# Four expert places of the second layer loaded in mid-mixer, between the ring's items

## The reference

```python
for l in range(DEPTH):                      # 2 layers
    hx = modulate(rmsnorm(x_lat, norm1_g[l]), sh1, sc1)      # latent tokens
    hc = modulate(rmsnorm(x_ctx, norm1_g[l]), csh1, csc1)    # context tokens
    # token mixer: keys and values from both, everything else of the last layer from hx alone
    dk, dv, nk, nv, dq, nq, pz, su, sv, gz = split_cols(hx @ w_in, COL_SIZES)
    dk_c, dv_c, nk_c, nv_c = split_cols(hc @ w_in[:, :KV_COLS], COL_SIZES[:4])
    ...                                     # four branches: pool, diff, sgu, na
    proj = einsum('btie,ied->btid', [pool_x, diff_x, sgu_x, na_x], w_br)
    mix = sum(sigmoid(gz) * proj, branches) @ w_out
    x_lat = x_lat + g1 * mix
    hx2 = modulate(rmsnorm(x_lat, norm2_g[l]), sh2, sc2)
    x_lat = x_lat + g2 * ec_moe(hx2, router_w[l], moe_w1[l], moe_w3[l], moe_w2[l])
    ...                                     # the context likewise, if l is not the last
```

## Time and profile before

| | |
|---|---|
| median of 3 runs | 2049.64 us (2046.07 to 2050.02) |
| profiled execution | 2047.61 us, its span 2045.8 us |
| granted TensorE clock, mean | 0.977 |
| PE busy | 1875.7 us (92%) |
| DVE / ACT / POOL busy | 696.7 / 443.1 / 119.0 us |
| HBM read | 563.11 MB, 276 GB/s over the span |
| chain that ended last | PE 66%, DMA 28%, DVE 3% |

### The profile page before, as it was taken

The page is one execution under the profiler, slowest core; times in us unless marked ns, Lnnn a source line. Parts: engine busy times, 40 slices in busy tenths (PEclk is TensorE's granted clock), DMA queues, the critical chain, the costliest instruction groups (busy, mean ns, idle before and its releaser), DMA issues.

```text
span 2045.8 us, 27379 instructions
## 1 busy us (share of the span) xinstructions
PE 1875.7 (92%) x11512; PEld 1096.7 (54%) x11512; DVE 696.7 (34%) x1149; ACT 443.1 (22%) x774; POOL 119.0 (6%) x159
## 2 busy tenths in 40 slices
PE   5999999999999899999889799999998887988787
PEld 3788756667788433333323488877896222222222
DVE  3263354654333422222212444467555010101001
ACT  3322243443222200000000332344433000000000
POOL 2080000000000100000000232000000000000000
PEclk9999999999999999999999899999998999999989
DMA  9423333344447799999999853444679999999997
GB/s 316 137 89 93 90 116 103 119 132 129 147 134 279 315 410 428 429 428 429 428 429 428 254 151 92 124 146 135 210 241 395 406 427 428 427 428 429 428 428 297
DMA packets 206319, 565.58 MB, mean 276 GB/s; under 512 B 9144, under 2 KB 156752, under 8 KB 180880
## 3 DMA queue, kind: packets, MB, share of 16 engines
q1 hardware_dynamic: 203920, 557.72, 70.6%
q0 software_dynamic: 1760, 4.40, 1.2%
q10 hardware_dynamic: 544, 2.10, 0.3%
HBM read 563.11 MB, written 1.07 MB: 276 GB/s over the span
## 4 chain that ended last, share of the span: by engine, by line
PE 66%; DMA 28%; DVE 3%; issue 1%; SPq 1%; ACT 1%; POOL 0%; DVEq 0%; ACTq 0%
PE PS L837 42%; PE PS L1280 16%; DMA e_h<-in_moe_w 13%; DMA arena<-in_moe_w 12%; DMA ring_par<-in_w_mod 2%; PE PS L893 2%; PE PS L1018 1%; PE PS L1223 1%; PE PS L1040 1%; DMA ring_par<-in_w_in 1%; SPq L773 0%; PE PS L1156 0%; PE PS L905 0%; PE PS L1250 0%; POOL small L1716 0%
## 5 line engine op out<-in xcount | busy, mean ns | idle before, releaser
L837 PE MATMUL PS<-hTr,wr 128*128 128x512 f32 (+1 forms) x2688 | 515.5, 348 | 9.6 <-DMA cst<-in_cst 4.4
L837 PEld LDWEIGHTS PS<-hTr,wr 128*128 128x128 f32 x2688 | 428.6, 190 | 77.0 <-issue 6.3
L1280 PE MATMUL PS<-e_h,arena 128*32 128x512 f32 x1312 | 270.1, 619 | 34.4 <-DMA arena<-in_moe_w 16.8
L1280 PE MATMUL PS<-arena 128*32 128x512 f32 x1216 | 264.0, 613 | 27.6 <-DMA arena<-in_moe_w 24.1
L1745 DVE TENSOR_TENSOR wr<-ring_par,wr 128x1024 fp32r<-128x1024 f32 x152 | 189.2, 1245 | 235.2 <-ACT wr L1351 234.9
L1351 ACT ACTIVATE wr<-ring_par 128x1024 fp32r<-128x1024 f32 x152 | 160.5, 1056 | 297.8 <-PE PS L837 268.3
L1280 PE MATMUL PS<-arena,nab 128*32 128x512 f32 x1088 | 199.6, 596 | 9.1 <-DMA arena<-in_moe_w 7.9
L837 PE MATMUL PS<-wr,hTr 128*128 128x512 f32 x816 | 187.5, 390 | 0.0
L837 PEld LDWEIGHTS PS<-wr,hTr 128*128 128x128 f32 x816 | 152.1, 188 | 32.5 <-DVE wr L1745 1.3
L2188 DVE TENSOR_TENSOR x_work<-x_work,PS 128x512 f32<-128x512 f32 x80 | 50.7, 684 | 345.5 <-PE PS L837 345.5
L1280 PEld LDWEIGHTS PS<-e_h,arena 128*32 128x32 f32 x1312 | 73.9, 113 | 168.4 <-issue 154.5
(11 more groups left out here) (193 smaller groups left out, 1647.7 us busy)
## 6 DMA issues: line engine op xcount, KB each, us to landing
arena<-in_moe_w SPq DMA_DIRECT2D x92, 2048.0 KB, 17.3
e_h<-in_moe_w SPq DMA_DIRECT2D x59, 2048.0 KB, 19.0
ring_par<-in_w_in SPq DMA_DIRECT2D x136, 512.0 KB, 4.1
e_wr<-in_moe_w SPq DMA_DIRECT2D x30, 2048.0 KB, 18.0
ring_par<-in_w_mod SPq DMA_DIRECT2D x92, 512.0 KB, 5.2
ring_par<-in_w_br SPq DMA_DIRECT2D x64, 256.0 KB, 4.6
ring_par<-in_w_out SPq DMA_DIRECT2D x16, 512.0 KB, 3.8
ring_par<-in_moe_w SPq DMA_DIRECT2D x4, 2048.0 KB, 16.7
```

The source lines that it names most:

```text
L837: return nc.tensor.matmul(o, a, b, start=first, stop=last)
L1280: ins = nc.tensor.matmul(PS[r:r + CAP, bank + h, :], src[:, k, r:r + CAP], space[:, kk * D + h * 512:kk * D + (h + 1) * 512], start=(k == ...
```

## The change

Only the second layer changes. A list `EARLY_LOADS` names four pieces that are issued inside the mixer's ring, each right behind the chunk that belongs to its unit: n = 5 in unit 2, n = 2 in unit 18, n = 8 in unit 21, n = 0 in unit 26. Each waits for what last used its memory: n = 5 for the key and value chunks, n = 2 and 8 for the end of the attention (`pv`), n = 0 for the 24th projection. n = 1 stays behind `w_out`, with the wait on the low parts of the merged sums (`m_lo`).

So that these places are free, the second layer lays `hTr` out by stream (the latent tokens fill one half, the context's the other; `by_stream`, `tokens_of`, `stream_of`), puts the rounded high parts of branches 2 and 1 in the unused upper columns of units 0 and 1, those of branch 3 in `x_work` (`x_work_r`, where the attention's buffer was), and the merged sums in the unused columns of units 2 and 3. The number and the sizes of the instructions on PE, DVE and ACT stay as they were.

```diff
+EARLY_LOADS = ((), ((2, 5), (18, 2), (21, 8), (26, 0)))
...
+KV_CHUNKS = 4 * (1 + max(i for i, g in enumerate(GROUPS) if g[0] in KV))
...
-        br_hi_of = {i: arena_r[:, u, :].rearrange("p (k t) -> p k t", k=4) for i, u in split_hi.items()}
+        br_hi_of = [{i: arena_r[:, u, :].rearrange("p (k t) -> p k t", k=4) for i, u in split_hi.items()},
+                    {2: arena_r[:, 0, :].rearrange("p (k t) -> p k t", k=4)[:, :, T:],
+                     1: arena_r[:, 1, :].rearrange("p (k t) -> p k t", k=4)[:, :, T:],
+                     3: x_work_r[:, 4 * D + 4 * 512:4 * D + 6 * 512].rearrange("p (k t) -> p k t", k=4)}]
...
-        mT = [x_flat[:, :].rearrange("p (k t) -> p k t", k=KD), x_flat[:, 2 * D:].rearrange("p (k t) -> p k t", k=KD)]
+        mT = [x_flat[:, :].rearrange("p (k t) -> p k t", k=KD),
+              unit_of(2, 2).rearrange("p (k t) -> p k t", k=KD)[:, :, T:]]
+        by_stream = hTr[:, :, :, :].rearrange("p a k t -> p (a k t)").rearrange("p (s a k t) -> p s a k t", s=2, a=2, k=KD)
+
+        def tokens_of(l, part, k, t0, t1):
+
+            if l == 0:
+                return hTr[:, part, k, t0:t1]
+            if t1 - t0 > T:
+                return by_stream[:, :, part, k, :]
+            return by_stream[:, t0 // T, part, k, t0 % T:t0 % T + t1 - t0]
...
-                    if first and turn == 0:
+                    if first and turn == 0 and l == 0:
                         sync.wait_ge(*(projs.at(l, NM) if s < EARLY_SLOTS else mix_sum.at(l, 2 * NT[l])))
+                    elif first and turn == 0:
+                        sync.wait_ge(*(projs.at(l, 3 * KD), m_lo.at(l, KD), pv.at(l, NB[l]), mix_sum.at(l, 2 * NT[l]),
+                                       mix_sum.at(l, 2 * NT[l]), chunk_sum.at(l, KV_CHUNKS))[s])
...
                     else:
                         sync.wait_ge(*pv.at(l, NB[l]))
-                        sync.wait_ge(*m_lo.at(l, KD))
                     sync.dma_start(xspace[e], rows_of(0, n)).then_inc(extra_loaded[e], 16)
...
+                early = EARLY_LOADS[l]
+                for unit, n in early:
+                    upto = [m for m, it in enumerate(items) if it[:3] == ("chunk", l, NW + unit + 2)][0] + 1
+                    load_items(at_item, upto)
+                    at_item = upto
+                    if n < ESLOT:
+                        load_slot(0, n, True)
+                    else:
+                        load_extra(n)
+                load_items(at_item, late)
+                at_item = end
+                done_early = [n for _, n in early]
                 for n in range(EARLY_SLOTS):
-                    load_slot(0, n, True)
-                if EXTRA[l] > 2:
-                    load_extra(ESLOT + 2)
+                    if n not in done_early:
+                        load_slot(0, n, True)
                 load_items(late, end)
                 load_late(l)
                 for n in range(EARLY_SLOTS, ESLOT):
-                    load_slot(0, n, True)
+                    if n not in done_early:
+                        load_slot(0, n, True)
...
```

More of the change, by code:

```diff
@@ L263, in build @@
         par = ring_par[:, NSLOT * 1024:NSLOT * 1024 + P_ALL]
+        with ExitStack() as rounded:
+            x_work_r = sb("x_work_r", [128, 4 * D + 9 * 512], f32r, rounded)
+            arena_r = sb("arena_r", [128, 8, 2048], f32r, rounded)
+            nab_r = sb("nab_r", [128, 8 * 6 * GRID_W], f32r, rounded)
         x_work = sb("x_work", [128, 4 * D + 9 * 512])
@@ L266, in build @@
         work = x_work[:, 4 * D:].rearrange("p (a b) -> p a b", a=9)
-        with ExitStack() as rounded:
-            arena_r = sb("arena_r", [128, 8, 2048], f32r, rounded)
-            nab_r = sb("nab_r", [128, 8 * 6 * GRID_W], f32r, rounded)
         arena = sb("arena", [128, 8, 2048])
@@ L323, in build, with stream_of @@
         x_flat = x[:, :, :].rearrange("p a b -> p (a b)")
-        mT = [x_flat[:, :].rearrange("p (k t) -> p k t", k=KD), x_flat[:, 2 * D:].rearrange("p (k t) -> p k t", k=KD)]
+        mT = [x_flat[:, :].rearrange("p (k t) -> p k t", k=KD),
[7 more added lines that the diff above has]
+            return by_stream[:, t0 // T, part, k, t0 % T:t0 % T + t1 - t0]
+        def stream_of(l, part, ks, s):
+            return hTr[:, part, ks, s * T:(s + 1) * T] if l == 0 else by_stream[:, s, part, ks, :]
         g1b = unit_of(6).rearrange("p (a b) -> p a b", a=2)
@@ L756, in _ @@
                 late = end - NSLOT * len(late_mod(l))
-                load_items(at_item, late)
-                at_item = end
                 G = GE[l]
@@ L965, in _ @@
                             i = three(bank[:, 0:u["tokens"]], wr[:, q % 2, 0, k * 128:(k + 1) * 128],
-                                      wr[:, q % 2, 1, k * 128:(k + 1) * 128], hTr[:, 0, k, 0:u["tokens"]],
-                                      hTr[:, 1, k, 0:u["tokens"]], k == 0, k == KD - 1, False)
+                                      wr[:, q % 2, 1, k * 128:(k + 1) * 128], tokens_of(l, 0, k, 0, u["tokens"]),
+                                      tokens_of(l, 1, k, 0, u["tokens"]), k == 0, k == KD - 1, False)
                         i.then_inc(chunk_sum.sem, 1)
@@ L1079, in _ @@
                                 i = three(PS[:, 5, 0:tok], wr[:, j % 2, 0, k * 128:(k + 1) * 128],
-                                          wr[:, j % 2, 1, k * 128:(k + 1) * 128], hTr[:, 0, k, 0:tok],
-                                          hTr[:, 1, k, 0:tok], k == 0, k == KD - 1, False)
+                                          wr[:, j % 2, 1, k * 128:(k + 1) * 128], tokens_of(l, 0, k, 0, tok),
+                                          tokens_of(l, 1, k, 0, tok), k == 0, k == KD - 1, False)
                             if arg == 1:
@@ L1117, in output @@
                         i = three(PS[:, 2 * m + n, :], wr[:, j % 2, 0, n * 512:(n + 1) * 512],
-                                  wr[:, j % 2, 1, n * 512:(n + 1) * 512], hTr[:, 0, k, m * 128:(m + 1) * 128],
-                                  hTr[:, 1, k, m * 128:(m + 1) * 128], k == 0, k == KD - 1, True)
+                                  wr[:, j % 2, 1, n * 512:(n + 1) * 512], tokens_of(l, 0, k, m * 128, (m + 1) * 128),
+                                  tokens_of(l, 1, k, m * 128, (m + 1) * 128), k == 0, k == KD - 1, True)
                         if k == KD - 1:
@@ L1381, in part_high @@
                     s, kp, _ = pairs[t]
-                    nc.scalar.activation(hTr[:, 0, 2 * kp:2 * kp + 2, s * T:(s + 1) * T],
+                    nc.scalar.activation(stream_of(l, 0, slice(2 * kp, 2 * kp + 2), s),
                                          htmp[:, t % 4, :].rearrange("p (k t) -> p k t", k=2), ACT.Copy)\
@@ L1507, in branch_high @@
                             act.wait_ge(*projs.at(l, HALF))
-                    nc.scalar.activation(br_hi_of[b][:, k, 0:tok], branches[:, b, k, 0:tok], ACT.Copy)\
+                    nc.scalar.activation(br_hi_of[l][b][:, k, 0:tok], branches[:, b, k, 0:tok], ACT.Copy)\
                         .then_inc(branch_hi.sem, 1)
@@ L1549, in _ @@
                     act.wait_ge(*chunk_sum.at(l, NW + NM))
-                    nc.scalar.activation(hTr[:, 0, k, 0:tok], mT[l][:, k, :], ACT.Copy, scale=0.5).then_inc(m_hi.sem, 1)
+                    nc.scalar.activation(tokens_of(l, 0, k, 0, tok), mT[l][:, k, :], ACT.Copy, scale=0.5).then_inc(m_hi.sem, 1)
                     if k == 1:
@@ L1801, in part_low @@
                     dve.wait_ge(*h_hi.at(l, t + 1))
-                    nc.vector.tensor_tensor(hTr[:, 1, 2 * kp:2 * kp + 2, s * T:(s + 1) * T],
+                    nc.vector.tensor_tensor(stream_of(l, 1, slice(2 * kp, 2 * kp + 2), s),
                                             htmp[:, t % 4, :].rearrange("p (k t) -> p k t", k=2),
-                                            hTr[:, 0, 2 * kp:2 * kp + 2, s * T:(s + 1) * T].bitcast(f32),
+                                            stream_of(l, 0, slice(2 * kp, 2 * kp + 2), s).bitcast(f32),
                                             ALU.subtract).then_inc(h_lo.sem, 1)
@@ L2007, in merged_low @@
                     dve.wait_ge(*m_hi.at(l, k + 1))
-                    nc.vector.scalar_tensor_tensor(out=hTr[:, 1, k, 0:tok], in0=mT[l][:, k, :], scalar=0.5,
-                                                   in1=hTr[:, 0, k, 0:tok].bitcast(f32), op0=ALU.mult,
+                    nc.vector.scalar_tensor_tensor(out=tokens_of(l, 1, k, 0, tok), in0=mT[l][:, k, :], scalar=0.5,
+                                                   in1=tokens_of(l, 0, k, 0, tok).bitcast(f32), op0=ALU.mult,
                                                    op1=ALU.subtract).then_inc(m_lo.sem, 1)
```

8 lines of the change are left out of this document (4 added, 4 removed).

## The result

| | before | changed |
|---|---|---|
| median of 6 runs each, taken together | 2046.59 us (2045.38 to 2050.02) | 2054.65 us (2053.84 to 2060.78) |
| ratio, 95% interval | | 1.0045, 1.0032 to 1.0057 |
| profiled execution, its span | 2047.61, 2045.8 us | 2060.78, 2059.0 us |
| granted TensorE clock, mean | 0.977 | 0.973 |
| PE / DVE / ACT / POOL busy | 1875.7 / 696.7 / 443.1 / 119.0 us | 1877.3 / 696.9 / 443.4 / 118.9 us |

The changed kernel is slower by 8 to 9 us. The direction was forecast, and 2054.65 lies 1.2 us from the forecast 2053.5. That distance flatters the forecast: it started from a median of 2049.64 and added 3.9 us, while the step really measured is about twice that (9.2 us by the ratio), from a lower start, 2046.59. The profiled execution of the changed kernel is the slowest of its six.

The account below looks back on a forecast made before the run. PE bounds the mixer and transfers the experts. Price 6.4 plus clock 1.8 less gain 4.3 is +3.9 us, from 2049.64 to 2053.5 us; range 2044.5 to 2060.

Parts of the forecast that it names:

- the hole: Between mixer and experts, 1595 to 1600 us, transfers at 211 GB/s: the only slack the change can reach.
- the stalls are hidden: Rival: pieces share engines with small items or PE finds slack, only the gain is left, -4.3 us, 2045.3; chance 0.22.
- transfers the only bound: Rival: naive 19.6 us less a price of 8.2, -11.4 us, 2038, with PE starting experts ten us sooner; chance 0.07.
- SP stands before a piece: Rival: SP waits before a piece whose memory is busy, result like rival 2; chance 0.21 shared with rival 2.
- Rival 2: Pieces hold up more, queue not recovering between units 18 and 21, clock falling twice: about +9 us, 2058.5; shared chance 0.21.
- The price in the mixer: Second layer's mixer: PE stalls at items behind early pieces, 0.3 + 1.2 + 4.9 = 6.4 us.
- Unit 2: Mixer: `mod` item lands at 1342.7 with the piece ahead, PE uses it at 1342.61; stall 0.3 us (0 to 1).
- Unit 18: Mixer: piece has a head start, `mod` item lands at 1472.5, PE wants it at 1471.28; stall 1.2 us (0 to 2).
- Unit 21: Mixer: no slack at the `mod` item, so the piece's full 4.9 us are a stall (4.0 to 5.5).
- Unit 26: Mixer: no `mod` item; branch item lands near 1514.7, ACT takes it at 1513.96; nothing taken, up to 1.5 us.
- The clock: Behind unit 21's stall the clock falls to half speed: 1.8 us (0 to 3.0); unit 18's stall costs none.
- The gain: At the hole: SP issues the tenth piece at 1594.8, so the experts' transfers start 4.3 us earlier (3.7 to 5.1).

Follow-up runs that it names:

- e5: Kernel before plus one early piece alone, n = 8 in unit 21 ahead of the `mod` item: 2051.63 us, ratio 1.0016.
- e9: Changed kernel with only unit 18's piece (n = 2) loaded early, the other eight where they stood before: 2045.58 us, ratio 0.9994.
- e3: Changed kernel with only unit 26's early piece (n = 0), where no `mod` item follows: 2044.74 us, ratio 0.9985.
- e4: Kernel before, without early pieces, second layer's gate vector read back behind the tenth and eleventh piece: 2041.83 us, ratio 0.9983.
- e11: The changed kernel run and profiled a third time, unchanged: single time 2055.32 us.
- e8: The changed kernel run and profiled a second time, word for word the same: 2056.45 us, ratio 1.0036 against the kernel before.
- e1: Changed kernel's layout alone, no early pieces, all nine first pieces behind the output projection as before: 2046.3 us, ratio 1.0000.
- e12: The kernel with only unit 21's early piece (e5) run once more, unchanged: single time 2049.32 us.
- e6: Changed kernel with each early piece issued one item later, behind its unit's `mod` item (unit 26 as it was): 2056.34 us, ratio 1.0039.
- e2: Changed kernel without unit 21's piece; three early pieces in units 2, 18 and 26: 2048.03 us, ratio 1.0013 against the kernel before.

## Why the prediction was right, and which step failed

**The bound and the mechanism: right.** PE in the mixer and transfers in the experts, a queue that lands its transfers in the order of issue, no slack at unit 21, and a gain limited to the hole. Each has a run of its own: e5 the wait at unit 21, e9 the recovery that the forecast claimed between units 18 and 21, e3 and e4 the hole. Of rivals, "the stalls are hidden" falls with e5, and "transfers the only bound" with P, which is later and not earlier. "SP stands before a piece" falls with SP's timeline: the piece is issued 0.41 us behind its chunk. Rival 2 named the size of the step, +9 us, but not the cause: no backlog reaches unit 21 (e9), and behind unit 26's branch item PE waits at most 0.57 us. Its second fall of the clock did come in the changed kernel's first execution.

**The failed step: "The price in the mixer", 6.4 us.** The direction and the range held, but this term of the sum was too small. The waits grew by 7.9 to 12.1 us in the three executions (8.99 to 13.17, less 1.07). The step took 2.097 MB / 428 GB/s = 4.9 us as what a piece holds back. That rate had been read where nothing but pieces moves. Among the ring's items it is the best case. Between its chunk's landing and its own, 5.8, 5.9 and 6.2 us passed in unit 2 of the three executions, 6.7, 5.5 and 5.0 in unit 18, and 7.6, 6.4 and 4.9 in unit 21. Term by term:
- Unit 2: 2.0, 1.75 and 1.97 us with the branch item, against 0.3 and above the end of 1. The piece's issue also takes 0.63 us of SP's time between the chunk and the `mod` item, which the step had not counted. The rest is the slower queue.
- Unit 18: 3.71, 2.25 and 2.22, against 1.2. The ends of the term were 0 and 2, and all three lie outside. Even at 5.0 us for the piece the wait was 2.2 (e11), because the chunk ahead landed 6.5 us after its issue instead of 5.8.
- Unit 21: 7.42, 6.90 and 4.80, against 4.9. The upper end of 5.5 is missed twice.
- Unit 26: 0.37 to 0.57 us ahead of a projection, against 0, within the end of 1.5.

**The clock: right behind unit 21, too small in all.** The next `mod` item comes 6.70 us after the late one (1502.00 to 1508.70) instead of some 5.1: 1.6 us, against 1.8. But the sum gave the shorter stalls no clock, and in the first execution 0.50 stands behind the waits of units 2 (1.70 us) and 18 (3.71 us) as well:
```profile
1345.50:1348.50 3.00, 3.00 (x9) 1.43 (x7) 0.42 (x1) 0.00 (x0) 0.00 (x0) 0.50 0.31 93
1478.50:1481.50 3.00, 3.00 (x17) 3.00 (x15) 0.02 (x1) 0.94 (x2) 0.00 (x0) 0.50 0.36 114
```
PE's busy time from A to B tells what the clock took in all, since its matmuls are the same. Before and changed:
```profile
1326.36:1560.36 234.00, 227.31 (x1754) 188.97 (x1753) 147.26 (x246) 103.51 (x202) 2.96 (x2) 1.00 0.62 202
1325.40:1576.60 251.20, 232.12 (x1754) 192.32 (x1753) 147.42 (x246) 103.71 (x202) 2.96 (x2) 0.97 0.65 213
```
That is 4.8 us, and 3.6 in e8 (230.88) and 2.6 in e11 (229.93). Not all of it need be the pieces' doing: e3 and e4, without a long wait at a ring item, have 1.5 and 1.3 us too, with the clock at 0.50 near 1400 and 1395, and e8 has such a stretch near 1400.

**The gain: near.** 4.3 us forecast. The tenth piece lands 4.1 to 5.8 us earlier after P, by before and e1 against the three executions; the end comes 2.9 to 4.6 us earlier after P. The signs on the transfers came out as written: the tenth piece issued at 7.09 and landed at 14.8 us, and the transfers nearly idle for the 8 us ahead of it (68 GB/s). PE's start of the experts, measured from A, moved by 9.8 to 17.2 us against the kernel before, where 6 to 10 was forecast.

**The sum with measured terms**, of the middle execution: waits 11.46 - 1.07 = 10.4, clock 3.6, other short gaps 0.3, so A to B grows by 14.3 us. The gain is 458.1 - 455.2 = 2.9, which makes +11.4. From B to P this execution is 3.3 us shorter than the one before, which the change doesn't explain. With that, A to the end is 8.2 us longer, and 14.2 and 6.5 in the other two. The ratio of 1.0045 is +9.2, in the midst of them; single executions don't fix it closer. The prediction's sum had +3.9, so it was right in sign and under half in size. What kept 2054.65 so near to 2053.5 was the start, 3.1 us too high.

**The rule weighed** (the Trainium skill, "DMA: Bandwidth & Descriptors", Specifications: transfers of 512 B and above move at line rate). Going against it was right for the chunks, and I should have gone further. The time of the piece behind the chunks was longer than 428 GB/s make it too: it was 5.5 us or more instead of 4.9 in nine of the twelve cases named here (three in unit 2, four in unit 18, five in unit 21). The changed kernel's 311 GB/s from 1494 to 1496, at a share of 0.96 and with no packet under 8 KB, stand against the rule.

**What stays open** is why the same piece takes 4.9 us in one execution and 7.6 in another. The share of busy DMA engines is nearly full in both. In the long cases small packets of later items move within that time, but whether they are its cause or come with it was not tried: no run here varied what else reads the memory, or the row length.

## What to carry to other kernels

A large transfer that is put among small ones in a queue served in order costs what the next needed item lacks in slack, and its time must be taken from rows of mixed traffic, with their spread, not from the rate of the stretch where it moves alone. Before moving several transfers, ask how many the hole can use. Here it was one, or none: reading the gate vector back behind two pieces gave the same gain (0.9983) without touching the mixer. And a difference between one profiled execution and another is to be measured again before a mechanism is built on it; two more executions here took away an explanation that had seemed half proven.

## What the runs showed that I had not expected

- The time of one 2 MB piece at the same place in the same kernel varied between executions (changed kernel 4.9 to 7.6 us, e5 and e12 4.9 and 6.5), at a nearly full share of the DMA engines. The two stretches of 2 us in which e5's piece moved have 426 and 410 GB/s:
```profile
1482.00:1484.00 2.00, 1.82 (x16) 1.62 (x14) 1.69 (x2) 0.14 (x1) 0.00 (x0) 1.00 1.00 426
1484.00:1486.00 2.00, 0.00 (x0) 0.00 (x0) 0.00 (x0) 1.19 (x2) 0.00 (x0) 0.99 0.96 410
```
- SP's own issue instruction takes long while much is queued: 5.13 us for the `mod` item issued at 1494.29, where the usual one takes 0.34 to 0.58. The branch item behind it was issued at 1499.47, right at its end; no wait of PE shows that this cost anything.
- The low clock can follow short waits too, at once, later or not at all: 2.39 and 3.85 us in e6 were followed by rows of 1.08 us at once; behind 1.70 and 3.71 us in the changed kernel and 2.17 in e2 the first row took 0.64 to 0.66 us and the clock fell 0.5 to 2 us after its start; behind 2.18 us in e9 it stayed at 1.00.
